# Sample caches in a decoder step: two tokens to a partition, two pages side by side

## The chip, the cores and the metric

The kernel runs on one core of one Trainium2 chip. The metric is the device time of one execution in microseconds. Before the change the median of three runs is 3156.51 us (3156.3 to 3161.36).

## What is computed

One step of a two-layer decoder for a prompt group (one sequence of 512 tokens) and a sample group (8 sequences with one new token each and 2048 past tokens in paged caches). Layer 0 mixes sparse attentions, layer 1 is a short gated convolution. The change touches the attention of the samples only. There each sample has a page table of 16 pages of 128 tokens; a page of a cache holds, for each token, 2 groups of 128 float32 values (1 KB a token, 128 KB a page):

```python
def gather_rows(pool, page_table, new, s, g):
    ...
    page = page_table[b_idx, sp // ps]
    from_pool = pool[page, sp % ps, g]
...
def gathered_attention(q, t, kg, vg, s, tbl):
    logits = jnp.einsum('bqgrd,bqgnd->bqgrn', q, kg, preferred_element_type=jnp.float32) * (q.shape[-1] ** -0.5)
    ...
    p = masked_softmax(logits + jnp.moveaxis(bias, -1, 3), (n >= 0)[:, :, :, None, :])
    return jnp.einsum('bqgrn,bqgnd->bqgrd', p.astype(vg.dtype), vg)
```

Three branches attend for the samples: `win` (a window of the last 512 tokens, from a dense state), `slc` (selected blocks) and `dsa` (tokens picked by an indexer). The kernel does not gather rows: for slc and dsa it reads all 16 pages, and a mask of -1e30 takes out what isn't selected.

## The kernel before

The program is a row of stages with a barrier of all engines behind each (L102). The stage in question is `stage_attend_samples` (from L1298). Its data are `fills` of 1 MB: 4 for win keys, 16 for slc keys, 16 for dsa keys, then 16 for slc values, 4 for win values, 16 for dsa values. Fill n goes to slot n mod 8; a slot holds 128 partitions x 8 pages x 256 values. Even fills are issued by SyncE (SP, from L1394), odd ones by ScalarE (ACT, from L1629). A fill of slc or dsa is eight transfers of one page each (`load_pages`, L905; its transfer is L913): token p of the page to partition p, 1 KB each. A fill of win is two transfers of 512 KB (L1387). Before it reuses a slot, the issuing engine waits (in `fill`, L1375) until the pages in it are turned (keys) or used (values); the wait for it is counted at L908, where the page numbers are loaded.

For **keys** TensorE goes through the samples in order. `turn_keys` (L1473) transposes two pages at a time, for both groups (four transposes, L1486), into one of the PSUM banks 3 and 4; VectorE's `keep_keys` (L1691, the copy is L1699) copies the bank into `kt`, the turned keys of two samples, [128 dims, 2, 2 groups, 2048 tokens]. TensorE may not write a bank again before its copy is done. When a sample's 8 pairs are copied, `add_logits` (L1489, the products are L1494) multiplies them by the queries; the logits of a sample lie in the order of the tokens, in four rows of partitions with 512 tokens each. TensorE turns the next sample's pages before it adds a sample's logits. Bias and masks are added in the order of the tokens too.

Beside the next kind's keys the softmax of a kind is worked out: maxima, exponentials (`exponentials`, L1616, into `p`), sums. Then `turn_probabilities` (L1510, transposes at L1516) turns each 128 tokens of `p` into PSUM, so that tokens lie on the partitions, and VectorE's `place` (L1736, copies at L1747) puts them into `pts`, one block of 32 columns for each sample and page.

For **values** `add_values` (L1523, the products are L1536) takes, for each page, its block of probabilities (128 partitions x 32) and the page as it lies in its slot (128 partitions x 256), and adds up; VectorE copies the sum of a sample (`keep_out`, L1755), TensorE turns it (`turn_out`, L1543), and VectorE adds it to the output (`add_out`, L1767, L1769). The next stage attends for the prompt.

Which token of a page lies on which partition matters in three places only: the transposed keys must come into `kt` in the order of the tokens, the block of probabilities must have its tokens on the partitions on which the values' tokens lie, and both must agree for the two pages of a pair. The pages of the other stages (`cz_pg`, `is_pages`) are loaded with `load_pages` as well. Names in other stages that the rows speak of: `xn` is the prompt's input (8 KB in each of 128 partitions), `w` with `in_w_ada` a weight in rows of 2 KB, `hot` a table of 32 partitions x 8.4 KB (loaded at 1043.5 us), `y_ring` a state of 16 partitions x 8 KB, and L1171 a copy of ScalarE, into `cz_xt` with a step of 128 elements between neighbours, into `cz_sums` without a step.

Of the kernel before, what the change touches and what calls it, by code (L numbers as in the profile page):

```python
# [19 lines left out]
P = 128  # L20
# [8 lines left out]
G = 2  # L29
# [3 lines left out]
PG = 16  # L33
NPOOL = 160
# [870 lines left out]
def load_pages(k, sp, cache, dst, arrived, s, first, count):  # L905


    _, pages = k.nc.values_load_multi_w_load_instructions(k.pages[0:1, bass.ds(s * PG + first, count)], engines=[sp.engine], min_val=0, max_val=NPOOL - 1,  # L908
                                                          skip_runtime_bounds_check_because="a page table holds numbers of pages of the pool only")
    for g, page in enumerate(pages):  # L910
        src = cache[0, bass.ds(page, 1)]
        src = src.rearrange("o p g d -> (o p) (g d)") if len(src.shape) == 4 else src.rearrange("o p d -> (o p) d")
        sp.dma_start(dst[:, g, :], src).then_inc(arrived, 16)  # L913


def load_w1(k, eng, which):

    eng.dma_start(k.w1[which], k.i["cmp_w1_" + which][0].rearrange("(l d) n -> d l n", d=P)).then_inc(k.w1_in[which], 16)
# [95 lines left out]
SLOTS = 8  # L1014
# [283 lines left out]
def stage_attend_samples(k):  # L1298
# [5 lines left out]
    nc, ps = k.nc, k.psum  # L1304
# [13 lines left out]
    arrived = k.arrived  # L1318
# [21 lines left out]
    with ExitStack() as ctx:  # L1340
# [34 lines left out]
        def fill(eng, n):  # L1375
            if n >= SLOTS:

                kind, kv, f = fills[n - SLOTS]
                if kv == 0:
                    eng.wait_ge(turned, chunk0[kind] + 4 * f + 4)  # L1380
                else:
                    eng.wait_ge(vused, run0[kind] + (2 * f + 2 if kind == "win" else f + 1))
            kind, kv, f = fills[n]
            name = INFO[kind][2 + kv]
            if kind == "win":
                for i in range(2):
                    eng.dma_start(slot(n)[:, 4 * i:4 * i + 4, :], k.i[name][0, 2 * f + i].rearrange("(n p) g d -> p n (g d)", p=P)).then_inc(arrived[n % SLOTS], 16)  # L1387
            else:
                load_pages(k, eng, k.i[name], slot(n), arrived[n % SLOTS], f // 2, f % 2 * 8, 8)

        with nc.Block() as block:

# [18 lines left out]
            def _(pe):  # L1411
# [98 lines left out]
                def turn_probabilities(kind):  # L1510

                    pe.wait_ge(prob[kind], 2)
                    to = logits(kind)
                    for sh in range(2):
                        for b in range(width(kind) // P):
                            mm = pe.transpose(to[:, sh, b * P:(b + 1) * P], p[:, sh, b * P:(b + 1) * P], k.ident)  # L1516
                    mm.then_inc(pt_mm[kind], 1)
                    pe.wait_ge(diag[kind], 2)
                    for sh in range(2):
                        mm = pe.transpose(ps[0:NS, MISC[kind], 148 + 32 * sh:180 + 32 * sh], pd[:, KINDS.index(kind), sh, :], k.ident[0:32, 0:32])  # L1520
                    mm.then_inc(pt_mm[kind], 1)
# [120 lines left out]
            def _(dve):  # L1642
# [48 lines left out]
                def keep_keys(kind, s):  # L1691
                    tb, u = INFO[kind][1] // 2, KINDS.index(kind) * NS + s
                    if u >= 2:

                        dve.wait_ge(used, u - 1)
                    for c in range(tb):
                        q = chunk0[kind] + s * tb + c
                        dve.wait_ge(turned, q + 1)
                        dve.tensor_copy(kt[:, s % 2, :, c * 256:(c + 1) * 256], ps[:, 3 + q % 2, :].rearrange("p (g q) -> p g q", g=G)).then_inc(kept, 1)  # L1699

                def own_tops(kind):
                    i = KINDS.index(kind)
# [990 lines left out]
```

## Time and profile before

| | |
|---|---|
| median of three runs | 3156.51 us |
| the profiled execution | 3156.13 us |
| its span | 3154.5 us |
| TensorE busy | 2898.6 us (92%) |
| VectorE busy | 1363.6 us (43%) |
| ScalarE busy | 771.5 us (24%) |
| moved | 496.82 MB, 157 GB/s over the span |
| the samples' stage, about | 1480 to 1737 us |

The profile is one execution. PE is TensorE, PEld its loads of weights, DVE VectorE, ACT ScalarE, POOL GpSimd, SP SyncE; a q behind a name is the engine's queue of instructions that aren't computation. A busy PE is not one at its peak, and PEclk is the share of full speed that its clock was granted (0.50 is 1.2 GHz, 1.00 is 2.4 GHz). DMA share is the mean busy share of the 16 engines that move data; above 1 means that packets overlap. In the counts of packets "under 2 KB" includes the ones "under 512 B". A wait is put down to what ended it last in the records.

### The profile page before, as it was taken

What the parts mean: (1) busy time and instruction counts of PE and PEld (TensorE: products, weight loads), DVE (VectorE), ACT (ScalarE), POOL (GpSimd) and SP (SyncE); (2) the same over time, 40 slices, a digit from 0 to 9 for tenths busy, and PEclk for the clock granted to TensorE, in tenths of its full rate; (3) what the DMA queues carried; (4) which work ended last, traced back from release to release, by engine and by line L of the source; (5) the groups of instructions that cost most, each with busy time, mean ns of one, the idle gap of its engine ahead of it and who ended that gap; (6) DMA issues with size and microseconds to landing.
All of it is one profiled execution on the core that took longest, in us unless ns stands there. A gap on an engine that the chain in (4) does not pass through costs nothing. (4 is left out here: it accounts for less than half of the span.)

```text
span 3154.5 us, 56117 instructions
## 1 busy us (share of the span) xinstructions
PE 2898.6 (92%) x22142; PEld 2561.1 (81%) x22142; DVE 1363.6 (43%) x2212; ACT 771.5 (24%) x1066; POOL 132.1 (4%) x150
## 2 busy tenths in 40 slices
PE   7699999999996779998888886997999999999897
PEld 4499999999995458886554565997999999999897
DVE  1422242222243628787661577335433443343434
ACT  2211222112121124442000454222222222222212
POOL 0000031000041000000000000000000000000000
PEclk8799999999998989998996898998999999999898
DMA  9766666767654743443889536432333333333421
GB/s 334 237 182 193 193 213 212 229 211 220 202 178 129 214 151 110 138 139 92 248 269 327 176 108 192 117 93 69 89 95 100 100 88 107 90 98 103 118 81 54
DMA packets 594875, 496.82 MB, mean 157 GB/s; under 512 B 37148, under 2 KB 515885, under 8 KB 593885
## 3 DMA queue, kind: packets, MB, share of 16 engines
q1 hardware_dynamic: 525800, 406.28, 43.5%
q10 hardware_dynamic: 61104, 62.69, 6.2%
q0 software_dynamic: 7840, 26.10, 2.2%
q8 instruction: 83, 1.36, 0.2%
q14 instruction: 48, 0.39, 0.0%
HBM read 459.95 MB, written 48.70 MB: 161 GB/s over the span
## 5 line engine op out<-in xcount | busy, mean ns | idle before, releaser
L146 PE MATMUL psum<-h_high,w_high 128*128 128x260 f32 x4992 | 1009.5, 283 | 21.5 <-DVE w_low L133 21.5
L146 PE MATMUL psum<-h_high,w_low 128*128 128x260 f32 x4992 | 1007.1, 283 | 0.0
L146 PE MATMUL psum<-h_low,w_high 128*128 128x260 f32 x4992 | 1005.3, 283 | 0.0
L146 PEld LDWEIGHTS psum<-h_high,w_high 128*128 128x128 f32 x4992 | 770.8, 189 | 35.9 <-issue 30.1
L146 PEld LDWEIGHTS psum<-h_high,w_low 128*128 128x128 f32 x4992 | 770.8, 189 | 0.0
L146 PEld LDWEIGHTS psum<-h_low,w_high 128*128 128x128 f32 x4992 | 769.1, 189 | 0.0
L133 DVE TENSOR_TENSOR w_low<-w,w_high 128x2048 fp32r<-128x2048 f32 x162 | 371.7, 2295 | 549.3 <-ACT w_high L128 549.3
L128 ACT ACTIVATE w_high<-w 128x2048 fp32r<-128x2048 f32 x162 | 309.2, 1909 | 467.5 <-PE psum L146 370.7
L628 DVE COPY pj_out<-psum 128x260 f32<-128x260 f32 x66 | 28.3, 429 | 381.9 <-PE psum L146 381.9
L576 ACT ACTIVATE pj_out<-psum 128x260 f32<-128x260 f32 x66 | 25.6, 388 | 584.7 <-PE psum L146 584.7
L1171 ACT ACTIVATE cz_xt<-psum 128x512 f32<-128x512 f32 x128 | 131.5, 1058 | 148.8 <-PE psum L1122 139.1
L199 PE MATMUL psum<-w,c 128*32 128x512 f32 x768 | 104.7, 658 | 26.2 <-DMA w<-in_w_ada 17.6
L1096 PE MATMUL psum<-w,cz_xt 128*128 128x256 f32 x512 | 123.3, 381 | 0.0
L1096 PE MATMUL psum<-w_v,cz_xt 128*128 128x256 f32 x512 | 122.8, 383 | 0.0
L1699 DVE COPY at_kt<-psum 128x512 f32<-128x512 f32 x144 | 93.2, 686 | 35.4 <-PE psum L1486 34.5
L1096 PEld LDWEIGHTS psum<-w_v,cz_xt 128*128 128x128 f32 x512 | 93.4, 193 | 10.3
L1096 PEld LDWEIGHTS psum<-w,cz_xt 128*128 128x128 f32 x512 | 92.4, 192 | 9.7
L2241 DVE TENSOR_TENSOR ou_t<-psum,adaT 128x8 f32<-128x8 f32 x32 | 5.3, 165 | 197.8 <-PE psum L146 184.5
L2519 DVE RECIPROCAL cv_parts<-cv_parts 128x520 f32<-128x520 f32 x16 | 54.5, 3404 | 71.9 <-ACT cv_parts L2454 71.9
L1122 PE MATMUL psum<-const,cz_pg 128*128 128x128 f32 x512 | 75.7, 277 | 9.2 <-ACT cz_xt L1171 9.2
L1910 PE MATMUL psum<-pa_k,pa_q 128*128 128x128 f32 (+3 forms) x192 | 74.7, 478 | 7.7 <-DVE pa_st L1989 4.0
L1122 PEld LDWEIGHTS psum<-const,cz_pg 128*128 128x128 f32 x512 | 63.5, 143 | 21.4 <-ACT cz_xt L1171 10.6
(333 smaller groups left out, 2640.7 us busy)
## 6 DMA issues: line engine op xcount, KB each, us to landing
w<-in_w_ada SPq DMA_DIRECT2D x96, 1024.0 KB, 7.9
w<-in_w_in_att SPq DMA_DIRECT2D x65, 1024.0 KB, 11.6
w<-in_w_in_conv SPq DMA_DIRECT2D x64, 1024.0 KB, 6.2
proj<-pj_out POOLq DMA_DIRECT2D x66, 260.0 KB, 4.8
cz_pg<-in_cache_nsa_cmp_k SPq DMA_DIRECT2D x128, 128.0 KB, 2.2
cz_pg<-in_cache_nsa_cmp_v SPq DMA_DIRECT2D x128, 128.0 KB, 2.1
w<-in_w_out_att SPq DMA_DIRECT2D x16, 1024.0 KB, 6.4
w<-in_w_out_conv SPq DMA_DIRECT2D x16, 1024.0 KB, 5.9
```

Of the source, the lines that this page charges most:

```text
L128: act.activation(k.wh[:, s % 2, :], k.w[:, n % 4, :], ACT.Copy).then_inc(self.high, 1)
L133: dve.tensor_tensor(k.wl[:, s % 2, :], k.w[:, n % 4, :], k.wh[:, s % 2, :].bitcast(F32), ALU.subtract).then_inc(k.w_free[n % 4], 1)
L146: mm = pe.matmul(k.psum[:, banks + hf, 0:HC], w[:, kt, :], x[:, kt, hf * HC:(hf + 1) * HC], start=(kt == 0 and m == 0), stop=(kt == KT - 1 ...
L199: mm = pe.matmul(k.psum[32 * a:32 * a + 32, self.bank, :], k.c32[:, q * 4 + a, :], k.w[:, n % 4, a * 512:(a + 1) * 512], start=(q == 0), s ...
L576: nc.scalar.activation(out[:, t % 4, 0:HC], ps[:, t % 2 * 2, 0:HC], ACT.Copy).then_inc(kept_a, 1)
L628: dve.tensor_copy(out[:, t % 4, HC:TC], ps[:, t % 2 * 2 + 1, 0:HC]).then_inc(kept_v, 1)
L1096: return pe.matmul(ps[:, m % 2, 0:CH], xt[:, m % 2, l, :], k.w1[which][:, l, :], start=(l == 0), stop=(l == CB - 1))
L1122: mm = pe.transpose(ps[:, 4 + c % 2, g * 256 + q * P:g * 256 + (q + 1) * P], pg[:, hf, 2 * c + q, g * P:(g + 1) * P], k.ident)
L1171: return nc.scalar.activation(o, i, ACT.Copy)
L1699: dve.tensor_copy(kt[:, s % 2, :, c * 256:(c + 1) * 256], ps[:, 3 + q % 2, :].rearrange("p (g q) -> p g q", g=G)).then_inc(kept, 1)
L1910: pe.matmul(ps[:, t % 2, 0:P * (i + 1)], hq[:, r % SL, i * P:(i + 1) * P], hk[:, r % SL, br, 0:P * (i + 1)], start=True, stop=True).then_i ...
L2519: dve.reciprocal(e[:, :], e[:, :]).then_inc(zrecip, 1)
```

## The change

The page transfers of this stage get a function of their own. A page is now laid out as 64 rows of two neighbouring tokens, 2 KB each, and goes to 64 partitions: even pages of a fill to partitions 0 to 63, odd ones to 64 to 127, into the columns of two pages. So partition m of the lower half holds tokens 2m and 2m + 1 of the even page, partition 64 + m those of the odd page; "page" column 0 of the pair holds the even tokens of both pages, column 1 the odd ones. When the keys are turned, a block of 128 columns is then every second token of 256. The copy into `kt` puts the two blocks back between each other with a step of two elements (slc and dsa; win is as before). The transposes of the probabilities read `p` with a step of two, so that each block has the tokens that lie on the partitions. The number and order of all transfers and instructions, slots, banks and waits are the same. The loads of the other stages still go through `load_pages`.

```diff
+def load_page_pairs(k, eng, cache, dst, arrived, s, first, count):
+
+    _, pages = k.nc.values_load_multi_w_load_instructions(k.pages[0:1, bass.ds(s * PG + first, count)], engines=[eng.engine], min_val=0, max_val=NPOOL - 1,
+                                                          skip_runtime_bounds_check_because="a page table holds numbers of pages of the pool only")
+    pairs = dst.rearrange("p (a e) d -> p a (e d)", e=2)
+    for g, page in enumerate(pages):
+        src = cache[0, bass.ds(page, 1)].rearrange("o (p e) g d -> (o p) (e g d)", e=2)
+        eng.dma_start(pairs[g % 2 * 64:g % 2 * 64 + 64, g // 2, :], src).then_inc(arrived, 16)
...
-                load_pages(k, eng, k.i[name], slot(n), arrived[n % SLOTS], f // 2, f % 2 * 8, 8)
+                load_page_pairs(k, eng, k.i[name], slot(n), arrived[n % SLOTS], f // 2, f % 2 * 8, 8)
...
-                            mm = pe.transpose(to[:, sh, b * P:(b + 1) * P], p[:, sh, b * P:(b + 1) * P], k.ident)
+                            at = slice(b // 2 * 256 + b % 2, (b // 2 + 1) * 256, 2) if kind != "win" else slice(b * P, (b + 1) * P)
+                            mm = pe.transpose(to[:, sh, b * P:(b + 1) * P], p[:, sh, at], k.ident)
...
-                        dve.tensor_copy(kt[:, s % 2, :, c * 256:(c + 1) * 256], ps[:, 3 + q % 2, :].rearrange("p (g q) -> p g q", g=G)).then_inc(kept, 1)
+                        to, own = kt[:, s % 2, :, c * 256:(c + 1) * 256], ps[:, 3 + q % 2, :]
+                        if kind == "win":
+                            dve.tensor_copy(to, own.rearrange("p (g q) -> p g q", g=G)).then_inc(kept, 1)
+                        else:
+                            dve.tensor_copy(to.rearrange("p g (m e) -> p g e m", e=2), own.rearrange("p (g e m) -> p g e m", g=G, e=2)).then_inc(kept, 1)
```

## Rows read from the trace of the kernel before

**Rows 1.** The page, part 1: busy us (share of span) and instructions per engine

```profile
PE 2898.6 (92%) x22142; PEld 2561.1 (81%) x22142; DVE 1363.6 (43%) x2212; ACT 771.5 (24%) x1066; POOL 132.1 (4%) x150
```

**Rows 2.** Timeline, end of the stage: start us, us, engine, line, operation [idle]

```profile
1736.18 0.29 DVE L1767 COPY oS<-psum 128x32 f32<-128x32 f32 x2 [1.37 <-PE psum L1543]
...
1737.63 0.15 POOL L2079 MEMSET pa_cm<- 128x64 f32 x1 [257.43 <-POOLq L102]
```

**Rows 3.** Stretches: length, busy (instructions) of five engines, PEclk, DMA share, GB/s

```profile
1506.00:1641.00 135.00, 118.13 (x914) 68.89 (x914) 91.85 (x164) 2.80 (x12) 0.00 (x0) 0.97 0.84 258
1541.24:1548.73 7.49, 6.54 (x50) 3.78 (x49) 5.15 (x9) 0.00 (x0) 0.00 (x0) 1.00 0.95 302
1650.00:1731.00 81.00, 73.07 (x583) 34.21 (x582) 12.02 (x39) 0.00 (x1) 0.00 (x0) 0.71 1.09 345
1045.00:1045.80 0.80, 0.80 (x6) 0.53 (x5) 0.80 (x2) 0.00 (x0) 0.00 (x0) 1.00 0.71 238
30.00:35.00 5.00, 5.00 (x23) 3.34 (x24) 0.49 (x2) 0.00 (x0) 0.00 (x0) 0.50 1.05 388
10.00:20.00 10.00, 7.30 (x47) 2.55 (x46) 0.00 (x0) 1.00 (x3) 0.00 (x0) 1.00 1.04 404
```

**Rows 4.** Transfers: 1650 to 1731 us in 40 slices; 1506 to 1641; window fills

```profile
GB/s 351 357 350 348 351 346 349 348 349 349 346 348 348 348 346 349 348 348 350 346 348 349 348 349 349 349 346 348 341 349 347 349 348 348 350 348 346 350 348 218
DMA packets 30179, 27.94 MB, mean 345 GB/s; under 512 B 3017, under 2 KB 30169, under 8 KB 30169
...
DMA packets 38082, 34.84 MB, mean 258 GB/s; under 512 B 4230, under 2 KB 38068, under 8 KB 38068
...
at_slots<-in_state_nsa_win_v SPq DMA_DIRECT2D x4, 512.0 KB, 14.9
```

**Rows 5.** Timeline of one sample of keys, 1541.24 to 1548.73 us

```profile
1541.24 1.92 PE L1494 MATMUL psum<-at_kt,qpa 128*32 128x512 f32 x16
...
1543.86 1.29 DVE L1699 COPY at_kt<-psum 128x512 f32<-128x512 f32 x2 [1.82 <-PE psum L1486]
...
1546.80 1.29 DVE L1699 COPY at_kt<-psum 128x512 f32<-128x512 f32 x2 [0.21 <-PE psum L1486]
...
1548.73 1.92 PE L1494 MATMUL psum<-at_kt,qpa 128*32 128x512 f32 x16
```

**Rows 6.** Waits of SP's queue, 1480 to 1740 us: us in total, times, longest

```profile
SPq L908 <- PE psum L1486: 62.6, 18, 7.7
```

**Rows 7.** Waits for arrivals, 1706 to 1735 us: us in total, times, longest

```profile
PEld psum L1536 <- DMA at_slots<-in_cache_dsa_v: 5.0, 4, 2.3
...
PEld psum L1536 <- DMA w<-in_cache_dsa_v: 3.0, 2, 1.8
```

**Rows 8.** Packets in 1045.0 to 1045.8 us and in 30 to 35 us

```profile
DMA packets 36, 0.19 MB, mean 238 GB/s; under 512 B 10, under 2 KB 14, under 8 KB 14
...
DMA packets 971, 1.94 MB, mean 388 GB/s; under 512 B 32, under 2 KB 32, under 8 KB 970
```

**Rows 9.** Transfers of the whole run: queue, count, KB each, median us to landing

```profile
cz_pg<-in_cache_nsa_cmp_k SPq DMA_DIRECT2D x128, 128.0 KB, 2.2
...
y_ring<-in_state_conv ACTq DMA_DIRECT2D x1, 128.0 KB, 3.2
```

**Rows 10.** Groups: instructions by line, shapes, count, busy us, mean ns, idle before

```profile
L1699 DVE COPY at_kt<-psum 128x512 f32<-128x512 f32 x144 | 93.2, 686 | 35.4 <-PE psum L1486 34.5
...
L1755 DVE COPY at_o<-psum 128x256 f32<-128x256 f32 x24 | 10.2, 425 | 75.6 <-PE psum L1536 75.6
...
L1516 PE MATMUL psum<-const,at_p 128*128 128x128 f32 x18 | 3.5, 347 | 0.0
...
L1747 DVE COPY at_pts<-psum 128x128 f32<-128x128 f32 x16 | 3.3, 282 | 2.4 <-PE psum L1520 2.4
...
L1171 ACT ACTIVATE cz_sums<-psum 128x512 f32<-128x512 f32 x2 | 1.1, 594 | 19.3 <-PE psum L1091 19.3
...
L1171 ACT ACTIVATE cz_xt<-psum 128x512 f32<-128x512 f32 x128 | 131.5, 1058 | 148.8 <-PE psum L1122 139.1
```

## The prediction, made before the change was run

> **What bounds the kernel now.** I read the share of each engine first, then the 40 slices, then the waits, a table of stretches and the transfers by stretch, all around the stage that attends for the samples. The profiled execution took 3156.13 us, its span 3154.5 us, and the median of the three runs is 3156.51 us, so one sum serves for both. TensorE is busy for 92% of the span, but that is a mean over stages with different limits [rows 1]. The change touches one stage only, from about 1480 to 1737 us of the span, so I read that one. The stages stand one behind the other: GpSimd sits 257.4 us at the barrier of L102 until the stage is over, and the next stage starts at 1737.63 us, 1.5 us behind the start of this one's last copies [rows 2]. What this stage gains or loses, the kernel gains or loses.
>
> The stage has two parts. **Keys**, 1506 to 1641 us: 34.84 MB in 135 us, 258 GB/s, with the transfers' share at 0.84 [rows 3, 4]. In steady state one sample takes 7.49 us, from one block of L1494 to the next (1541.24 to 1548.73 us). Inside it TensorE turns two pages, VectorE copies them out of one of two banks (686 ns each), and the pairs of copies stand some 0.2 us apart; then TensorE adds the logits in 1.92 us while VectorE has nothing left but the next sample's first pair [rows 5]. The queue of SP waits 62.6 us in sum for slots that the turning frees [rows 6]. So here the copies set the pace and the transfers are made to wait, but not by much: in this very sample they run at 302 GB/s with a share of 0.95 [rows 3].
>
> **Values**, 1650 to 1731 us: 345 GB/s at a share of 1.09, and all slices but the last near 348 GB/s [rows 3, 4]. This part is bound by transfers from end to end. TensorE looks 73 of 81 us busy, but at a mean granted clock of 0.71; late in it, between 1706 and 1735 us, its weight loads wait 5.0 + 3.0 = 8.0 us for arrivals of dsa's values [rows 7]. The last pages arrive near 1731 us, and 5 us later the stage is done [rows 2].
>
> **What the change does, part by part.** (1) Each of 512 page transfers (4 caches x 8 samples x 16 pages) keeps its 128 KB, but becomes 64 rows of 2 KB into 64 partitions in place of 128 rows of 1 KB into 128; even pages go to the lower half of the partitions, odd ones to the upper. Number, order, slots, semaphores and queues stay. The rows say that 2 KB pieces alone are faster: w_ada, which comes in 2 KB rows over all 128 partitions, runs at 388 GB/s between 30 and 35 us, against 345 to 348 for the pages [rows 3, 4, 8]. Of the 27.94 MB of the values part 4.19 MB are the eight window fills of 512 KB (four on SP's queue, four on ACT's), which stay as they are [rows 4]. The other 23.75 MB take 68.8 us at 345 GB/s and would take 61.2 us at 388: **-7.6 us**. That is the whole prize. In the keys part a faster transfer only waits longer for its slot, so nothing comes from there. TensorE would have to keep up; the 8.0 us that it waits near the end [rows 7] are about as long as the gain, so it can, just.
>
> (2) Against it stands the half. Two rows of this trace bear on loads into part of the partitions. The table hot goes into 32 partitions in pieces of 8 KB; where it runs nearly alone (22 of 36 packets are of 8 KB and more) the rate is 238 GB/s, while x_prompt in the same piece size over all partitions, with w_ada's 2 KB pieces beside it, runs at 404 [rows 3]. And y_ring, 128 KB into 16 partitions, lands 3.2 us after its issue where 128 KB into all partitions land in 2.2 [rows 9]. So a single transfer into half the partitions is bound near 238 GB/s. Here halves alternate, page by page, and two queues issue side by side, so at times both halves are written at once. The rate then lies between 238 (all writers always on one half) and 388 (never). No row shows this alternation. Writers that find the other half in work as often as their own would see the mean of the two times per byte, 2/(1/238 + 1/388) = 295 GB/s; I take **300**. The values part then takes 23.75/300 = 79.2 us instead of 68.8: **+10.4 us**. In the keys part a sample of 2.1 MB needs 7.0 us at 300, still under 7.49; but the part runs at 302 when it is steady and above 320 where it catches up, so I add **+3 us** by eye, with 0 and +18 (see below) as its ends. At 238 both ends are dear; that is a rival.
>
> The Trainium skill (SBUF — State Buffer, Door 1: The DMA port swizzle) says that partitions 0 to 63 reach only 8 of 16 ports, measured at 196 GB/s, and that two transfers at once to the two halves gained only 6%. By it the rate would be some 208 GB/s and the values part 114 us, 45 us more; the row with 238 GB/s agrees in direction, but no row here shows two halves at once.
>
> (3) 128 of the 144 copies of L1699 (the 16 of win stay) read PSUM as before and write kt with a step of two elements. The path through a sample holds eight of them, so a copy that grows by d costs 8d per sample and 128d in all. A copy with runs of eight that are scattered over pages (L1747) takes 282 ns for 128 elements, where 256 plain ones take 425 and 512 take 686, no dearer per element; but ScalarE's L1171, which writes 512 elements each a row away from the last, takes 1058 ns where 512 in a row take 594 [rows 10]. So d lies between 0 and 464 ns, the cost between **0 and +59 us**, and nothing speaks for a gain. A step of two is a far smaller hop than L1171's 128 elements, so the plain copies are the nearer row: I take 0.
>
> The Trainium skill is of two minds: SBUF — State Buffer (Door 1) wants two hits to each 16-byte line, which a step of two in float32 gives; Vector Engine (DVE) Microarchitecture Reference (the SBUF access granule) has full rate only for runs of two adjacent words. By the first d is 0; by the second some 0.65 cycles an element, about 350 ns a copy and 44 us in sum.
>
> (4) 16 transposes of probabilities (L1516, slc and dsa) read p with a step of two. They take 347 ns in the mean [rows 10]; even doubled they would cost 5.6 us, half of it beside copies or arrivals. I take 0, and +3 for the range.
>
> Sum: 3156.1 + 10.4 + 3 = **3169.5, say 3170 us**.
>
> **The rivals.**
> *Faster: the halves don't meet.* Writers drift apart, or what they hold back covers the turns, and pages run at 388 GB/s. -7.6 us: 3148.5. For it: 2 KB pieces do run faster, and with two queues and 16 engines a lockstep is not bound to hold. Against it: hot and y_ring.
> *Slower still: the halves go in step.* All engines work on the same page at the same time, so half of SBUF's entrance is idle: 238 GB/s. Values 23.75/238 = 99.8 us, +31; a sample of keys takes 8.81 us instead of 7.49, some 14 of 16 samples +18. In all +49: 3205. It begins to bind the keys below 280 GB/s (2.1 MB in 7.49 us).
> *Slower by VectorE: the step costs.* With half of L1171's extra, 232 ns, it is +30; with all of it +59. If the transfers keep their gain that is +22 to +51, in the middle 3193. It decides from 60 ns a copy on, where 128d has eaten the 7.6 us. The keys' period would grow while the values stay.
> *A draw.* The rate comes out at 335 to 355 GB/s and the copies stay: nothing to see.
> That the edit is not in effect is no case: the built program has 64x512 in the place of 128x256.
>
> **How the numbers follow.** Chances: forecast (halves meet now and then, 270 to 335 GB/s) 0.34, no meeting 0.32, in step 0.12, the step costs 0.17, draw 0.05. A measurement can tell 0.2%, 6.3 us. The no-meeting case gains little more than that, so 0.05 of it counts as same; of the forecast 0.04 does. Faster 0.27, same 0.14, slower 0.59. The range has to hold both signs: from 3146 (the gain with 2 us to spare) to 3220 (in step with +15, or the step at its dearest). The forecast's own range is 3160 to 3185.
>
> **What would show it.** The rate in the 81 us before the stage's end: 388 is the rival, 300 the forecast, 238 the lockstep; the share of the transfers stays near 1 in all three. L1699's duration (686 ns) and the keys' period of 7.49 us tell of the step. The stage's end, now 1736 us, carries it all; every stage behind it must keep its length. The forecast is wrong if the values part gets shorter, or if the keys' period grows with the rate in it well below what the transfers can do.

## The result, and the profile after

| | before | after |
|---|---|---|
| median | 3156.63 us (4 runs) | 3177.53 us (4 runs; 3175.79 to 3179.63) |
| ratio to before | | 1.0064, 95% interval 1.0053 to 1.0076 |
| span of the profiled execution | 3154.5 us | 3174.1 us |
| GpSimd's wait at the barrier, the stage's length | 257.43 us | 278.15 us |

The change makes the kernel slower by 0.64%, 20.9 us. The two profiled spans differ by 19.6 us, and GpSimd's wait for the stage to end has grown by 20.7 us (257.43 in [rows 2]). So the whole loss lies in the stage that the change touches. The timeline of the kernel after, GpSimd's wait at its end and VectorE's last copies (start us, us, engine, line, operation, idle before; the code stands some 10 to 15 lines lower than before):

```profile
1754.87 0.42 DVE L1770 COPY at_o<-psum 128x256 f32<-128x256 f32 x1 [5.43 <-PE psum L1547]
1756.18 0.29 DVE L1782 COPY oS<-psum 128x32 f32<-128x32 f32 x2 [0.89 <-PE psum L1554]
```

```profile
1757.63 0.15 POOL L2094 MEMSET pa_cm<- 128x64 f32 x1 [278.15 <-POOLq L102]
```

The last copies were at 1736.18 us before [rows 2]. The stage itself begins within 1 us of where it began. To part it, I read the first product of the values in both traces. Timelines of TensorE, the kernel before and then the kernel after:

```profile
1641.67 1.93 PE L1536 MATMUL psum<-at_slots,at_pts 128*32 128x256 f32 x32
```

```profile
1643.85 1.93 PE L1547 MATMUL psum<-at_slots,at_pts 128*32 128x256 f32 x32
```

The values part, from its first product to the last copies, went from 94.5 to 112.3 us, 17.8 us more. Its first product comes 2.2 us later, or 2.9 us counted from the start of the stage (161.5 us before, 164.4 now). That is no more than single executions scatter by: in e1 and g2 below, whose keys are transferred as before the change, the same distance is 167.3 and 165.2 us. The table of stretches of after, with the columns of [rows 3]:

```profile
1506.00:1641.00 135.00, 117.85 (x921) 70.41 (x924) 93.29 (x166) 2.81 (x12) 0.00 (x0) 0.97 1.02 255
1650.00:1731.00 81.00, 71.70 (x498) 32.16 (x490) 10.74 (x36) 1.72 (x6) 0.00 (x0) 0.58 1.07 285
```

In the values' stretch the rate fell from 345 to 285 GB/s at nearly the same share (1.09 to 1.07): the engines that move data are as busy as before and move less. TensorE shows 71.7 of 81 us busy, and looks like the bound; but 498 of its instructions are recorded there where 583 were, at a mean granted clock of 0.58 in place of 0.71. It works at the low clock (1.2 GHz) more of the time and is a little more idle, and the busy share hides that. In the keys' stretch the rate is nearly the same, 255 for 258 GB/s, while the share rose from 0.84 to 1.02. Transfers in the whole stage, 1480 to 1765 us in 40 slices, the tenths of the share above the GB/s, and the landing times of dsa's pages:

```profile
DMA  6987996999999999999999999999999999999906
GB/s 192 245 215 202 247 236 171 247 244 248 247 248 261 264 271 281 267 277 266 260 279 264 261 242 234 252 267 275 302 340 271 296 295 300 304 305 302 284 12 202
...
at_slots<-in_cache_dsa_k SPq DMA_DIRECT2D x32, 128.0 KB, 6.9
...
w<-in_cache_dsa_v SPq DMA_DIRECT2D x32, 128.0 KB, 11.7
```

The same two kinds of transfers in the kernel before:

```profile
at_slots<-in_cache_dsa_k SPq DMA_DIRECT2D x32, 128.0 KB, 2.7
...
w<-in_cache_dsa_v SPq DMA_DIRECT2D x32, 128.0 KB, 8.1
```

A page of dsa's keys now lands 6.9 us after its issue, not 2.7, and one of dsa's values 11.7 us, not 8.1. In the slices of after, two beyond 300 GB/s in the middle (302, 340) are where window fills, which are as before, join in. The rate is not one number: the pages run at 234 to 275 GB/s in the six slices (7.1 us each) ahead of the window fills, and dsa's values, the last pages, at 295 to 305. VectorE's copies, grouped by line from 1480 to 1700 us, are the lines to hold against [rows 10]; L1714 is the copy with the step of two, L1712 the plain one of the window:

```profile
L1714 DVE COPY at_kt<-psum 128x512 f32<-128x512 f32 x128 | 82.6, 686 | 26.3 <-PE psum L1496 25.9
L1712 DVE COPY at_kt<-psum 128x512 f32<-128x512 f32 x16 | 10.7, 688 | 11.8 <-PE psum L1496 11.7
L1770 DVE COPY at_o<-psum 128x256 f32<-128x256 f32 x12 | 5.1, 425 | 43.0 <-PE psum L1547 43.0
L1762 DVE COPY at_pts<-psum 128x128 f32<-128x128 f32 x16 | 3.3, 279 | 2.5 <-PE psum L1531 2.5
```

And the period of a sample of keys, the blocks of L1504 (logits) in TensorE's timeline:

```profile
1542.33 1.92 PE L1504 MATMUL psum<-at_kt,qpa 128*32 128x512 f32 x16
1549.82 1.92 PE L1504 MATMUL psum<-at_kt,qpa 128*32 128x512 f32 x16
1557.30 1.92 PE L1504 MATMUL psum<-at_kt,qpa 128*32 128x512 f32 x16
```

The step of two costs VectorE nothing (686 ns before, 686 ns now), and the keys keep their 7.49 us.

### The profile page after: what moved, and what is told of

Read it like the earlier page. It is cut to its first block and busy times, and to the rows that moved or that the text cites. A ratio compares the mean times of both kernels' runs of the same rounds, so it can differ in the third digit from the quotient of the medians.

```text
span 3174.1 us, 56117 instructions
## 1 busy us (share of the span) xinstructions
PE 2909.9 (92%) x22142; PEld 2564.4 (81%) x22142; DVE 1363.6 (43%) x2212; ACT 771.0 (24%) x1066; POOL 131.9 (4%) x150
## 5 line engine op out<-in xcount | busy, mean ns | idle before, releaser
L1714 DVE COPY at_kt<-psum 128x512 f32<-128x512 f32 x128 | 82.6, 686 | 26.3 <-PE psum L1496 25.9
```

Of the source, the lines that this page charges most:

```text
L1714: dve.tensor_copy(to.rearrange("p g (m e) -> p g e m", e=2), own.rearrange("p (g e m) -> p g e m", g=G, e=2)).then_inc(kept, 1)
```

## The experiments

The theory is that writes into half of the partitions lower the rate, that the rate matters in the values part alone, and that 2 KB pieces would be a gain without the halves. The rivals are the step of two (in the copies or the transposes), the 2 KB pieces themselves, and a debt that slower keys leave for the values. Each kernel was timed in three rounds beside the kernel before; the ratio is to that. The edits are to the kernel after, but e3's is to the kernel before, and e4's is shown against e3. Each shows its main lines only; `...` marks what is left out, among it the number of arrivals that a slot waits for, which follows the number of transfers. The stage's length is GpSimd's wait at the barrier, in one profiled execution; it scatters by 4 us and more (two of the kernels below show 261 us at a ratio of 1.000, where before showed 257, and f1 shows 290.5 us at a ratio of 1.0073, where after showed 278.2 at 1.0064), so the medians carry the verdicts, and the rates the reasons.

### One part of the change alone

**The step without the new transfers** (`e1_step_only`). Pages come as before the change, 128 rows of 1 KB; copies and transposes keep the step of two.

```diff
-                load_page_pairs(k, eng, k.i[name], slot(n), arrived[n % SLOTS], f // 2, f % 2 * 8, 8)
+                load_pages(k, eng, k.i[name], slot(n), arrived[n % SLOTS], f // 2, f % 2 * 8, 8)
```

> The changed kernel with its pages loaded as before (128 rows of 1 KB over all partitions); copies and turns keep their step of two. It leaves out the laying side by side that makes the step right, so tokens come out in another order; the work is the same. My theory (the halves cost, the step does not): 3156 us within 3 us, copies of 683 ns, values part at 345 to 348 GB/s. Rival (the step costs): some 3170 or more.

Measured: 3158.42 us against 3159.3, ratio 0.9996 (0.9985 to 1.0007). The copies take 685 ns, and the values run at 348 GB/s again (1660 to 1720 us):

```profile
L1714 DVE COPY at_kt<-psum 128x512 f32<-128x512 f32 x128 | 82.6, 685 | 26.4 <-PE psum L1496 26.1
```

The interval ends at +2.2 us, so of the 20.9 us next to nothing is VectorE's or the transposes'.

**The halves without the 2 KB pieces** (`e2_halves_1k`). A page still goes to 64 partitions, but as two pieces of 1 KB for each.

```diff
-        src = cache[0, bass.ds(page, 1)].rearrange("o (p e) g d -> (o p) (e g d)", e=2)
-        eng.dma_start(pairs[g % 2 * 64:g % 2 * 64 + 64, g // 2, :], src).then_inc(arrived, 16)
+        src = cache[0, bass.ds(page, 1)].rearrange("o (e p) g d -> (o p) e (g d)", e=2)
+        eng.dma_start(pairs[g % 2 * 64:g % 2 * 64 + 64, g // 2, :].rearrange("p (e d) -> p e d", e=2), src).then_inc(arrived, 16)
```

> The changed kernel, but each page comes as 64 x 2 pieces of 1 KB (tokens m and 64 + m of a page to one partition), so the halves stay and the 2 KB pieces go; the order of the tokens in a block is then not the one that copies and turns assume. If the halves cost: as slow as the changed kernel or slower, since 1 KB pieces are slower by themselves: 3177 to 3200 us, under 300 GB/s in the values part. If it is the 2 KB pieces that are slow (reads from memory): back to 3156 us and 348 GB/s.

Measured: 3186.73 us, ratio 1.0094 (1.0071 to 1.0116); 278 GB/s in the stretch of the values, 240 in that of the keys. The halves cost 0.94% with the old pieces and 0.64% with the new ones: the halves are the loss, and the longer pieces give back some of it. The ratios put that at a third, 9.5 us, but their own intervals touch, and the difference may be anything from about 2 to 17 us.

**The 2 KB pieces without the halves** (`e3_all_partitions_2k`). A transfer carries 256 KB, 2 KB to each of 128 partitions, read in a row from a place in the pool that the number of the even page sets (not that page's own tokens, so the contents are left out); four transfers to a fill instead of eight, the copies and transposes plain as before the change.

```diff
...
+    for j in range(count // 2):
+        src = bass.AP(cache.tensor, pages[2 * j] * 16384, [[512, 128], [1, 512]])
+        eng.dma_start(dst[:, 2 * j:2 * j + 2, :].rearrange("p a d -> p (a d)"), src).then_inc(arrived, 16)
...
```

> The kernel before, its pages fetched as half as many transfers of 256 KB, 128 rows of 2 KB over all partitions (256 tokens in a row from a place that depends on the page number, not the page's own tokens: the contents are left out, the volume is the same). If the halves cost and 2 KB pieces gain: 385 GB/s in the values part and 3149 us (-7.6). If nothing is to be had from 2 KB pieces: 3156 us, or slower.

**The same transfers with 1 KB pieces** (`e4_all_partitions_1k`), for what half as many transfers give by themselves.

```diff
-        src = bass.AP(cache.tensor, pages[2 * j] * 16384, [[512, 128], [1, 512]])
-        eng.dma_start(dst[:, 2 * j:2 * j + 2, :].rearrange("p a d -> p (a d)"), src).then_inc(arrived, 16)
+        src = bass.AP(cache.tensor, pages[2 * j] * 16384, [[256, 128], [32768, 2], [1, 256]])
+        eng.dma_start(dst[:, 2 * j:2 * j + 2, :], src).then_inc(arrived, 16)
...
```

> As the kernel with 256 KB transfers, but each of them in 128 x 2 pieces of 1 KB: tells the size of a transfer from the size of its pieces. Theory: 348 GB/s and 3156 us within 3 us, as before the change. If it is the number of transfers that matters: as fast as its sister with 2 KB pieces.

Measured: e3 3150.72 us, 0.9974 (0.9963 to 0.9986); e4 3153.96 us, 0.9989 (0.9977 to 1.0000). Transfers of e3 and then of e4, 1660 to 1720 us:

```profile
GB/s 385 384 389 386 382 389 350 354 348 348 349 348 349 356 372 383 390 381 389 385 386 388 384 386 391 382 268 356 265 163 336 266 356 381 362 391 406 395 386 386
```

```profile
DMA packets 21455, 20.87 MB, mean 348 GB/s; under 512 B 1142, under 2 KB 21449, under 8 KB 21449
```

Over all partitions the 2 KB pieces run at 381 to 391 GB/s in most slices where no window fill joins in (there 348 to 354), and the kernel gains 8 us; with 1 KB pieces the rate is 348 as ever. So the pieces are good, at just the rate that w_ada had shown [rows 8]; what they lose in the kernel after comes with the halves. The intervals of e3 and e4 overlap, so it is the rates that tell the pieces from the count of transfers. The dips of e3's last third (163 to 268) are no limit of the transfers: SP's queue waits there for slots that TensorE has yet to use, and from 1697 to 1720 us TensorE is busy without a break, at a granted clock of 0.50. The waits of SP's queue from 1695 to 1715 us and that stretch (columns as in [rows 3]), both of e3:

```profile
SPq L918 <- PE psum L1545: 12.7, 3, 8.0
```

```profile
1697.00:1720.00 23.00, 23.00 (x161) 10.08 (x160) 1.99 (x6) 0.00 (x0) 0.00 (x0) 0.50 0.96 341
```

So TensorE's slack is used up in e3, as the prediction had it ("just"); that a still faster transfer would bring little follows from it, but was not run.

### Which part of the stage pays

**Keys alone, values alone** (`g1_keys_only`, `g2_values_only`). The new pages for one kind, the old ones with their plain copies or transposes for the other.

```diff
-                load_page_pairs(k, eng, k.i[name], slot(n), arrived[n % SLOTS], f // 2, f % 2 * 8, 8)
+                (load_pages if kv else load_page_pairs)(k, eng, k.i[name], slot(n), arrived[n % SLOTS], f // 2, f % 2 * 8, 8)
...
```

> The change for the keys alone: values come over all partitions in rows of 1 KB, and the turns of the probabilities have no step. My split says keys +3 and values +10 or, by the trace after, some +2 and +18. So 3157 to 3160 us here if each part pays for itself; up to 3167 if the keys' slower transfers leave the values with fewer full slots (a debt carried over), although the keys themselves end on time.

```diff
-                load_page_pairs(k, eng, k.i[name], slot(n), arrived[n % SLOTS], f // 2, f % 2 * 8, 8)
+                (load_page_pairs if kv else load_pages)(k, eng, k.i[name], slot(n), arrived[n % SLOTS], f // 2, f % 2 * 8, 8)
...
```

> The change for the values alone: keys and their copies as before, values by pairs, turns with their step. If each part pays for itself: 3172 to 3175 us; if the keys leave a debt: 3164 to 3170 us, and with the run for the keys alone the two add up to the change's 3177 or so.

Measured: keys alone 3157.38 us, 1.0003 (0.9991 to 1.0014); values alone 3179.19 us, 1.0078 (1.0053 to 1.0104). The stretches of g1, then those of g2 (columns as in [rows 3]):

```profile
1506.00:1641.00 135.00, 118.12 (x925) 70.00 (x927) 93.28 (x166) 2.80 (x12) 0.00 (x0) 0.97 1.01 254
1650.00:1731.00 81.00, 72.92 (x596) 33.93 (x592) 12.01 (x39) 1.72 (x6) 0.00 (x0) 0.69 1.09 346
```

```profile
1506.00:1641.00 135.00, 118.24 (x924) 70.95 (x922) 92.87 (x168) 2.80 (x12) 0.00 (x0) 0.96 0.88 253
1650.00:1731.00 81.00, 69.47 (x528) 32.36 (x520) 11.74 (x39) 1.72 (x6) 0.00 (x0) 0.68 1.07 287
```

In g1 the transfers of the keys' stretch are busy from end to end, at a share of 1.01, and deliver 254 GB/s; that is all that the keys need, for the copies set their pace and the stretch moved 258 GB/s before [rows 3]. Nothing is left over as a debt: its values part, first product to last copies, takes 95.6 us. That of g2, whose keys come as before, takes 112.4 us, like the kernel after's 112.3. The loss is in the values, all of it that these runs can tell. What was moved from the start of the stage to the first product of the values, in the kernel before and then in the kernel after, says the same of the slots, which are equally full at that point:

```profile
DMA packets 44630, 40.84 MB, mean 253 GB/s; under 512 B 4975, under 2 KB 44611, under 8 KB 44611
```

```profile
DMA packets 24713, 40.67 MB, mean 247 GB/s; under 512 B 4951, under 2 KB 4975, under 8 KB 24694
```

### What the rate of the halves hangs on

On both queues the kernel after has the order lower, upper, lower, upper. The next kernels change that order only; the same pages go to the same places.

**The two queues in opposite turns** (`f1_alternate_opposed`): ACT's queue begins with the upper half.

```diff
-    for g, page in enumerate(pages):
+    for g in ((1, 0, 3, 2, 5, 4, 7, 6) if eng.engine == k.nc.scalar.engine else range(8)):
+        page = pages[g]
```

> The changed kernel; ScalarE's fills issue the pages of each pair in the other order (upper half first), SyncE's as before. Same work and layout. If the rate hangs on how often both queues write the same half: something other than 3177 us, up or down by 5 us or more, with the rate in the values part moved from 300 GB/s. If each queue's alternation alone sets it, or the sum is a mean over drifting queues: 3177 within 4 us.

**Four pages in a row to a half** (`f2_one_half_in_a_row`), both queues alike.

```diff
-    for g, page in enumerate(pages):
+    for g in (0, 2, 4, 6, 1, 3, 5, 7):
+        page = pages[g]
```

> The changed kernel; each fill issues its four lower-half pages in a row, then its four upper-half ones, on both queues. Theory (a half alone takes some 238 GB/s, the mixture of halves takes more): the rate falls where both queues are on the same half, and the kernel gets slower, 3180 to 3200 us. Rival (what costs is 64 partitions to a transfer, whichever half): 3177 within 4 us.

**Four in a row, the queues on opposite halves** (`f3_halves_apart`). If two queues on two halves keep both busy, this was meant to be the kernel to show it.

```diff
-    for g, page in enumerate(pages):
+    for g in ((1, 3, 5, 7, 0, 2, 4, 6) if eng.engine == k.nc.scalar.engine else (0, 2, 4, 6, 1, 3, 5, 7)):
+        page = pages[g]
```

> The same, but ScalarE's fills issue the four upper-half pages first, SyncE's the four lower-half ones: as long as the queues keep step, one writes one half while the other writes the other. Theory: the rate rises towards 388 GB/s, 3150 to 3165 us, faster than the changed kernel. Rival (64 partitions to a transfer cost as such): 3177 within 4 us.

Measured: f1 3180.18 us, 1.0073 (1.0056 to 1.0090), by its time not to be told from the kernel after (its one profiled execution, the slowest of its four, shows lower rates, 274 GB/s for 285 in the values and 245 for 255 in the keys, so a small effect of the queues' turns is not excluded); f2 3191.34 us, 1.0107 (1.0090 to 1.0125); f3 3228.19 us, 1.0235 (1.0218 to 1.0253). Transfers of f2, 1660 to 1720 us, and of f3, 1540 to 1620 us:

```profile
GB/s 212 216 246 209 212 249 213 212 257 214 223 245 220 220 245 224 219 245 225 222 205 203 291 350 349 345 348 350 345 208 163 171 198 243 238 221 255 239 224 260
```

```profile
GB/s 209 219 215 219 213 212 214 209 216 212 201 223 204 216 212 202 225 206 214 219 206 227 207 225 211 212 225 205 217 217 211 217 204 220 213 212 221 205 231 212
DMA packets 10382, 17.12 MB, mean 214 GB/s; under 512 B 2068, under 2 KB 2068, under 8 KB 10373
```

All three read the same pages in the same pieces and write them to the same places as the kernel after, so what differs is the order, with it which half is written when, and not the pieces or the number of partitions of a transfer.

f3 fell the other way from what I expected: it is the slowest of the three, flat at 214 GB/s with a full share. But its queues did not do what the order was meant to bring. Fills are alike on both queues, 1.05 MB, first 0.52 MB to one half and then 0.52 MB to the other; so how far one queue is ahead says which half each one writes. What SP's queue (q1) and ACT's (q10) have moved between 1474 and 1640 us, in f3:

```profile
q10 hardware_dynamic: 10521, 17.26, 51.3%
q1 hardware_dynamic: 10864, 17.76, 51.2%
```

and in f2:

```profile
q1 hardware_dynamic: 11970, 19.58, 46.7%
q10 hardware_dynamic: 11580, 18.99, 46.0%
```

In both, SP's queue is ahead by about half a fill (0.50 and 0.59 MB). In f3, whose queues have opposite orders, that puts both on the *same* half; counted by the 2 KB packets of each queue, they are there for nine tenths of the time from 1540 to 1620 us. In f2, whose queues have the same order, it puts them on *different* halves, for four fifths of the time. And f2 runs faster there (1540 to 1620 us, at a share of 1.05):

```profile
DMA packets 12495, 20.58 MB, mean 257 GB/s; under 512 B 2495, under 2 KB 2495, under 8 KB 12486
```

Later in f2 the queues have drawn closer. Between 1474 and 1670 us they have moved:

```profile
q10 hardware_dynamic: 13869, 22.75, 47.4%
q1 hardware_dynamic: 14033, 22.97, 47.4%
```

That is 0.22 MB apart, a fifth of a fill: now both are on one half for some two thirds of the time. Here f2 falls to 212 GB/s, with peaks of some 250 every third slice, 4.5 us, where one queue has changed sides and the other has not (0.52 MB for each queue at 227 GB/s, the mean of the first 18 slices, take 4.6 us). So f3 measures one half, 214 GB/s, f2 measures both: some 250 to 257 GB/s when the queues are on different halves, 212 when they are on the same. So my theory stands in part: two halves at once are faster than one, but by a fifth, not up to 388 GB/s. Why they stop there is not shown. (The profiled execution of f2 is the slowest of its four, 13 us above the median.)

For the turns of one page, in the kernel after and f1, the same count does not work: a page is 64 packets, which dealt evenly over 16 engines is four each, and an engine that is a few packets ahead is already in the other half. That this spread is what lifts them to 285 GB/s is argued; no record shows which packet an engine has at a given moment.

f3 also shows a debt, which g1 had not. Up to the first product of its values it had moved this:

```profile
DMA packets 21917, 36.09 MB, mean 215 GB/s; under 512 B 4383, under 2 KB 4407, under 8 KB 21899
```

That is 4.75 MB less than before the change, 22 us at 214 GB/s. The keys hardly show it (the first product of the values comes 167.5 us after the stage's start, like e1's 167.3), but the values part takes 163.3 us in place of 94.5. So at 214 GB/s, well below the keys' mean of 258, the slots are used up, and the values pay for the keys as well as for themselves.

**A page over both halves** (`f4_both_halves_a_page`): two transfers for a page, 32 partitions in each half, 64 KB each. The turns are then as fine as they can be.

```diff
-        eng.dma_start(pairs[g % 2 * 64:g % 2 * 64 + 64, g // 2, :], src).then_inc(arrived, 16)
+        for h in range(2):
+            at = 64 * h + g % 2 * 32
+            eng.dma_start(pairs[at:at + 32, g // 2, :], src[32 * h:32 * h + 32, :]).then_inc(arrived, 16)
...
```

> The changed kernel with each page cut into two transfers of 64 KB, one to 32 partitions of the lower half and one to 32 of the upper half, pieces of 2 KB as in the change (tokens lie on other partitions than copies and turns assume; the work is the same). The halves alternate twice as finely. Theory in its simple form (the mean of meeting and not meeting): about as the changed kernel, 3170 to 3185 us; if finer turns are covered by what the transfer engines hold back: faster, 3150 to 3165 us; if the number of transfers costs: slower.

Measured: 3210.89 us, 1.0178 (1.0161 to 1.0195). Its transfers, 1540 to 1620 us:

```profile
DMA  6887775877788877588777777677777787867777
...
DMA packets 13503, 18.56 MB, mean 232 GB/s; under 512 B 4502, under 2 KB 4502, under 8 KB 13490
...
at_slots<-in_cache_dsa_k SPq DMA_DIRECT2D x64, 64.0 KB, 2.4
```

Another limit has come in: the share is 0.76 in the mean, so the engines that move data are not full, and a transfer lands after 2.4 us. SP's queue shows what it is; its issues, start us and us, 1540 to 1620 us:

```profile
1556.15 17.34 SPq L925 DMA_DIRECT2D at_slots<-in_cache_dsa_k  x32
1574.24 17.49 SPq L925 DMA_DIRECT2D w<-in_cache_dsa_k  x32
1592.46 16.44 SPq L925 DMA_DIRECT2D at_slots<-in_cache_dsa_k  x32
```

It issues 32 transfers of 64 KB every 18.1 us, about 0.55 us each, and in these 80 us waits only 2.2 us for slots. Two queues at that pace bring 2 x 2.1 MB in 18.1 us, 232 GB/s, which is the rate measured: in the keys f4 is bound by issuing. The packets under 512 B have nearly doubled (4502 against 2539 in the kernel after over the same 80 us), as the transfers have. So f4 says what twice as many transfers of half the size cost here, and nothing of finer turns.

**The middle half** (`g3_middle_half`): even pages to partitions 32 to 95 in one transfer, odd pages to 0 to 31 and 96 to 127 in two, so that every page reaches both halves with fewer small transfers than in f4.

```diff
-        eng.dma_start(pairs[g % 2 * 64:g % 2 * 64 + 64, g // 2, :], src).then_inc(arrived, 16)
+        for at, row, n in (((0, 0, 32), (96, 32, 32)) if g % 2 else ((32, 0, 64),)):
+            eng.dma_start(pairs[at:at + n, g // 2, :], src[row:row + n, :]).then_inc(arrived, 16)
...
```

> Even pages go to partitions 32 to 95 in one transfer of 64 partitions, odd ones to 0 to 31 and 96 to 127 in two of 32; pieces of 2 KB (tokens lie elsewhere than copies and turns assume, the work is the same). If it matters which partitions a transfer reaches (both of the two halves): half of the bytes at 388 GB/s, the rest at the 235 of the run with pages cut in two, 293 GB/s in all, 3175 to 3185 us. If it is the count of partitions: as slow as that run, 3205 us or more.

Measured: 3195.11 us, 1.0124 (1.0102 to 1.0146); 274 GB/s in the stretch of the values, 236 in that of the keys at a share of 0.87. This lies between what the two theories gave, so it decides nothing: faster than f4 by some 16 us with 12 transfers to a fill instead of 16, slower than the kernel after with its 8. In the keys the small transfers may bind as in f4 (SP's queue waits only 0.4 us for slots from 1540 to 1620 us); in the values the share is 1.08, so there the engines are full at 274 GB/s, where the theory of the halves had 293. What the middle half is worth stays open.

**The halves apart with 1 KB pieces** (`g4_halves_apart_1k`): f3's order, e2's pieces, to see whether f3's floor belongs to the packets or to the half.

```diff
-    for g, page in enumerate(pages):
-        src = cache[0, bass.ds(page, 1)].rearrange("o (p e) g d -> (o p) (e g d)", e=2)
-        eng.dma_start(pairs[g % 2 * 64:g % 2 * 64 + 64, g // 2, :], src).then_inc(arrived, 16)
+    for g in ((1, 3, 5, 7, 0, 2, 4, 6) if eng.engine == k.nc.scalar.engine else (0, 2, 4, 6, 1, 3, 5, 7)):
+        page = pages[g]
+        src = cache[0, bass.ds(page, 1)].rearrange("o (e p) g d -> (o p) e (g d)", e=2)
+        eng.dma_start(pairs[g % 2 * 64:g % 2 * 64 + 64, g // 2, :].rearrange("p (e d) -> p e d", e=2), src).then_inc(arrived, 16)
```

> The order of the run with halves apart, in pieces of 1 KB (again tokens m and 64 + m to a partition, contents out of place). If the flat 215 GB/s is what one half of SBUF takes, the size of the pieces hardly matters: 200 to 215 GB/s, 3228 to 3245 us. If it comes from overhead by piece, the rate falls in proportion as 348 to 388, to 193 GB/s, some 3260 us.

Measured: 3234.96 us, 1.0243 (1.0226 to 1.0260). Its transfers, 1540 to 1620 us:

```profile
DMA packets 18084, 16.57 MB, mean 207 GB/s; under 512 B 2001, under 2 KB 18075, under 8 KB 18075
```

207 against 214 GB/s, a ratio of 0.97, where over all partitions 1 KB pieces stand to 2 KB pieces as 348 to 388, 0.90. So near the floor the size of the pieces hardly counts, and the floor is no matter of overhead by piece. Here too the orders are opposite and SP's queue is ahead by 0.63 MB (17.15 against 16.52 MB between 1474 and 1640 us), six tenths of a fill, so that the queues are on the same half for some four fifths of the time. It is the half that takes no more than 207 to 214 GB/s. The Trainium skill gives 196 GB/s for a transfer into partitions 0 to 63 (SBUF — State Buffer, Door 1: The DMA port swizzle) and 6% more for two at once to the two halves (the same page, "Can I just issue two DMAs to hit both halves?"), by my estimate some 208. For one half f3 and g4 agree with it nearly (214 and 207 GB/s). For both halves f2 has more, 257 against f3's 214, a fifth and not 6%, and the kernel after with its turns page by page, 285 in the stretch, more still.

No kernel here is faster than the one before and still fetches the pages that the table names. Only e3 is clearly faster, by 0.26%, and it leaves them out: the pages of a pair don't lie side by side in the pool; a way to fetch two separate pages in 2 KB rows over all 128 partitions in one transfer was not run.

## Why the prediction was right, and where it was off

It said 3170 us, slower by halves that meet now and then; measured are 3177.53 us, inside the forecast's own range of 3160 to 3185.

- **What bounds the stage.** Right. The values go by transfers, and the keys do not at the change's rate; g1 and g2 part them cleanly (1.0003 and 1.0078). That it is VectorE's copies that pace the keys is read from the rows [rows 5]; no run made them slower or faster.
- **(1) The 2 KB pieces, -7.6 us.** Right: 388 GB/s was taken from w_ada's row, e3 shows 381 to 391 and a ratio of 0.9974, 8 us. On halves they are worth 9.5 us, within wide bounds (e2 against the kernel after, 2 to 17 us).
- **(2) The halves, +10.4 us in the values.** That halves cost was right, and the size short: the part grew by 17.8 us. The term was the rate. I took 300 GB/s; 23.75 MB in 68.8 + 17.8 = 86.6 us are 274. What was too high is the floor of one half, 238 GB/s, read from 0.8 us of hot's transfer, which goes into 32 partitions and has other packets beside it [rows 3, 8]. f2 and f3 show it at some 212 and 214, g4 at 207. With 214 my own formula, the mean of the two times per byte, gives 2/(1/214 + 1/388) = 276 GB/s, 86.1 us, +17.3. It fits, but it was worked out with the result in hand, and the formula's picture of writers that meet by chance is not shown by that: its other end, 388 GB/s for writers that don't meet, is not what f2 has with its queues on different halves, 257. So the sign is earned by the mechanism, but that 300 GB/s came near the 274 measured is in part luck. By the figures of the Trainium skill (SBUF — State Buffer, Door 1: The DMA port swizzle) I had estimated 208 GB/s and +45 us for the values: too dear for the kernel after (285 GB/s, +17.8 us). For f3, with both queues on one half, the rate is about right (214), the price too low: its values part grew by 68.8 us, 42 for its own bytes at 214 GB/s and 22 for the keys' debt.
- **The keys, +3 us.** The trace has 2.2, inside the scatter, and g1 has nothing (+0.6 us, interval -3 to +4), so the term should have been 0. The sentence that keys bind below 280 GB/s was wrong: I had divided one steady sample (2.1 MB in 7.49 us), but the stretch's mean need was 258 GB/s, since the keys also wait for products and softmax between the kinds, and the eight slots lend what a steady sample is short of. The kernel after holds 7.49 us in most samples with slices from 244 to 281 GB/s. Even at the 214 GB/s of f3 the slots carry the keys a long way: their period is about 7.5 us until 1611.91 us and then some 10, which is 2.1 MB at 214 GB/s. TensorE's timeline of f3, the logits of its last samples:

```profile
1604.38 1.92 PE L1505 MATMUL psum<-at_kt,qpb 128*32 128x512 f32 x16
1611.91 1.92 PE L1505 MATMUL psum<-at_kt,qpb 128*32 128x512 f32 x16
1622.43 1.92 PE L1505 MATMUL psum<-at_kt,qpb 128*32 128x512 f32 x16
1632.28 1.92 PE L1505 MATMUL psum<-at_kt,qpb 128*32 128x512 f32 x16
```
- **(3) The step of two, 0.** Right: 686 ns before and after, e1 at 0.9996. One reading on the way was loose: L1747's 282 ns for 128 elements are 2.2 ns an element, against 1.3 for the 512 plain ones, so it is "no dearer" only with a fixed part taken off (the line through 425 and 686 ns has 164 ns fixed and 1.02 ns an element, 294 ns for 128). Of the Trainium skill's two pages, SBUF — State Buffer (Door 1, two hits to a 16-byte line) agrees with the 686 ns; the granule of Vector Engine (DVE) Microarchitecture Reference, by which I had estimated 350 ns more a copy, does not show for this copy.
- **(4) The transposes, 0.** Right within e1's interval of 3.5 us.
- **The rivals.** That halves don't meet (3148.5 us) is what e3 shows without halves, so its price was right and its condition false. In step at 238 GB/s (3205) did not happen in the kernel after. f3 has that rival's condition, both queues on one half for nine tenths of the time, at a floor of 214: by the prediction's own sum +42 for the values and +32 for 14 samples of 9.8 us, 3230 in all, against 3228 measured.

## What to carry to other kernels

When an edit makes transfers' pieces longer, look at which partitions they land on: here 2 KB pieces were worth 8 us over 128 partitions, and the same pieces, page by page on 64, made the kernel 20.9 us slower. A rate for part of the partitions should be read from a steady transfer, not from a stretch of a microsecond, and the half that binds can be found with one kernel that puts the transfers in a row. Whether two queues are on the halves that the program means them to be has to be read from the bytes of each queue, not from the order of issue. A part of a stage that is paced by an engine tolerates slower transfers as long as its mean need, not that of its steadiest sample, is met: the share rises to 1 and the time stays (g1). Well below that mean the buffers run down, and the next part pays (f3). Before cutting transfers smaller, compare the pace at which a queue issues them with the pace at which the bytes are needed (f4).

## What the runs showed that I had not expected

- Order alone, with the same bytes, pieces and places, moves the rate in the keys from 262 GB/s (turns page by page, 1540 to 1620 us) to a flat 214 (four in a row, the two queues in opposite orders), in the values from 290 to 229 (1660 to 1720 us, window fills and all), and the kernel from 3177 to 3228 us. What the order sets is not all: in f3 half a fill between the queues turned opposite orders into the same half.
- Transfers of 64 KB into 32 partitions leave the 16 engines at a share of 0.76 (232 GB/s), although a transfer lands in 2.4 us, because two queues that issue one every 0.55 us bring no more; 256 KB instead of 128 KB into all partitions change nothing that can be told (e4, 0.9989).
- TensorE's mean granted clock in the values' stretch fell with the change, from 0.71 to 0.58, and to 0.52 in f3. It does not follow the rate strictly: g2 has 0.68 at 287 GB/s, f1 0.52 at 274. Its busy time there, 71.7 of 81 us, says nothing of the bound: it had fewer products in it than before.
- What stays open is why turns page by page reach 285 GB/s in the mean and 305 at best, above the 257 of two queues on different halves, why those stay so far below 388, and why the rate rises within the stage. That engines run a few packets apart is my guess; no run shows it.
